# Two layers of a hybrid backbone on one core: the first weight pieces converted earlier, tokens handed on in smaller parts, the last product and the last norm reordered

## The reference

```python
mod = jax.nn.silu(c) @ w_ada[l] + b_ada[l]            # one row of 6 * 1024 numbers per stream
sh1, sc1, g1, sh2, sc2, g2 = jnp.split(mod, 6, axis=-1)
out, k, v, h_fin = token_mixer(x * (1 + sc1) + sh1, ...)   # h @ w_in, then attention, SSD scan, gMLP
x = layer_norm(DEEPNORM_ALPHA * x + g1 * out, ln_g[l, 0], ln_b[l, 0])
ff = hier_moe(x * (1 + sc2) + sh2, ...)               # 32 experts, D_FF 256
x = layer_norm(DEEPNORM_ALPHA * x + g2 * ff, ln_g[l, 1], ln_b[l, 1])

def layer_norm(x, g, b):
    mu = jnp.mean(x, -1, keepdims=True)
    var = jnp.mean(jnp.square(x - mu), -1, keepdims=True)
    return (x - mu) * lax.rsqrt(var + LN_EPS) * g + b
```

## Time and profile before

| | us |
|---|---|
| median of 3 runs | 1404.84 |
| the profiled execution | 1404.46 |
| its span, first to last instruction | 1402.7 |
| PE busy | 1302.7 (93%) |
| DVE busy | 1000.5 (71%) |
| ACT busy | 733.8 (52%) |

### The profile page before, as it was taken

One profiled execution on the slowest core, in us unless ns is written; L12 is line 12 of the kernel. 1 busy time (PEld: TensorE's weight loads), 2 busy tenths in 40 slices (PEclk: granted clock), 3 DMA queues, 4 the chain that ended last, 5 costly groups with the idle time before them and its releaser, 6 DMA issues.

```text
span 1402.7 us, 17438 instructions
## 1 busy us (share of the span) xinstructions
PE 1302.7 (93%) x6480; PEld 1032.3 (74%) x6480; DVE 1000.5 (71%) x1129; ACT 733.8 (52%) x693; POOL 54.5 (4%) x89
## 2 busy tenths in 40 slices
PE   4799999999989999999969999999987999999994
PEld 1668777887677787887757777788776777788873
DVE  0555657667578888888867456666856888888886
ACT  0533543643356666667653444345434666676772
POOL 1301000001000000000020000000000000000000
PEclk8799999989879999999989989899986999999997
DMA  9968653326848989899967667343334898999991
GB/s 358 295 200 304 245 202 128 121 90 230 314 164 303 354 318 333 326 336 342 358 193 238 251 242 258 120 128 100 126 148 143 298 337 320 333 329 330 344 359 49
DMA packets 96275, 349.54 MB, mean 249 GB/s; under 512 B 8580, under 2 KB 12064, under 8 KB 79792
## 3 DMA queue, kind: packets, MB, share of 16 engines
q1 hardware_dynamic: 87216, 295.12, 59.1%
q0 software_dynamic: 8960, 53.16, 10.8%
HBM read 345.58 MB, written 3.70 MB: 249 GB/s over the span
## 4 chain that ended last, share of the span: by engine, by line
PE 70%; DVE 18%; DMA 4%; ACT 3%; issue 2%; DVEq 2%; SPq 1%; ACTq 0%
PE bank L856 66%; DVE wl L1657 9%; PE bank L859 4%; ACT wh L1577 1%; DMA first<-in_w_ada 1%; DMA raw<-in_moe_w 1%; DMA adaw<-in_w_ada 1%; DVE merged L1657 1%; DVE tmp L1657 1%; DVE x L1657 1%; DVE hid L2310 1%; ACT wh L1379 1%; DVE x L1781 0%; DVE gv L1657 0%; DVE xgl L2283 0%
## 5 line engine op out<-in xcount | busy, mean ns | idle before, releaser
L1657 DVE TENSOR_TENSOR wl<-raw,wh 128x2048 fp32r<-128x2048 f32 (+1 forms) x268 | 610.4, 2278 | 129.5 <-ACT wh L1379 66.7
L1577 ACT ACTIVATE wh<-raw 128x2048 fp32r<-128x2048 f32 x192 | 367.3, 1916 | 62.8 <-PE bank L856 47.1
L856 PE MATMUL bank<-wh,xgh 128*128 128x512 f32 x512 | 213.5, 417 | 10.3 <-DVEq L2284 7.0
L856 PE MATMUL bank<-wh,hTh 128*128 128x512 f32 (+1 forms) x480 | 199.2, 415 | 14.3 <-DVE wl L1657 7.6
L856 PE MATMUL bank<-wh,xgl 128*128 128x512 f32 x512 | 205.9, 402 | 0.0
L856 PE MATMUL bank<-wl,xgh 128*128 128x512 f32 x512 | 205.5, 401 | 0.0
L856 PE MATMUL bank<-wl,hTh 128*128 128x512 f32 (+1 forms) x480 | 193.7, 404 | 0.0
L856 PE MATMUL bank<-wh,hTl 128*128 128x512 f32 (+1 forms) x480 | 192.4, 401 | 0.0
L1379 ACT ACTIVATE wh<-raw 128x2048 fp32r<-128x2048 f32 (+1 forms) x76 | 142.2, 1872 | 79.2 <-PE bank L856 72.6
L856 PEld LDWEIGHTS bank<-wh,hTh 128*128 128x128 f32 x480 | 96.5, 201 | 37.3 <-DVE wl L1657 12.6
L856 PEld LDWEIGHTS bank<-wh,xgh 128*128 128x128 f32 x512 | 99.2, 194 | 30.5 <-issue 10.9
(11 more groups left out here) (277 smaller groups left out, 1591.0 us busy)
## 6 DMA issues: line engine op xcount, KB each, us to landing
raw<-in_moe_w SPq DMA_DIRECT2D x256, 512.0 KB, 4.9
raw<-in_moe_w SPq DMA_DIRECT2D x64, 1024.0 KB, 5.6
raw<-in_w_in SPq DMA_DIRECT2D x52, 1024.0 KB, 5.3
adaw<-in_w_ada POOLq DMA_DIRECT2D x32, 1024.0 KB, 7.1
raw<-in_w_branch SPq DMA_DIRECT2D x12, 1024.0 KB, 5.3
raw<-in_w_ada SPq DMA_DIRECT2D x8, 1024.0 KB, 11.1
raw<-in_w_o SPq DMA_DIRECT2D x8, 1024.0 KB, 4.8
first<-in_w_ada SPq DMA_DIRECT2D x4, 1024.0 KB, 16.7
```

The lines of the kernel that those rows point to most:

```text
L856: return behind(nc.tensor.matmul(*args, **kw))
L1577: tally(A_(wh[c][:, :], raw[:, r, :], ACT.Copy), part_high[c])
L1657: return V.tensor_tensor(o, a, b, op)
```

## The change

It has five parts.

1. Layer 0: ACT converts q piece 0 before `take_row` and q piece 1 right behind it, both ahead of the modulation. DVE converts q piece 0 before its modulation and q piece 1 behind the low parts of the first half.
2. The first half of stream 0 is handed on in two parts of two blocks (the diff calls them by first and end): `hT_ready` is raised 5 times a layer, and TensorE waits for the second part only before its third block. In layer 1, DVE puts these two low parts between the statistics of stream 1.
3. The last expert's turned rows have a buffer of their own (`hTTh1`, `hTTl1`), and the columns of `down(30)` are split: the first 512 before `turn_hidden(31)`, the others behind it.
4. Change of layer: ACT converts q piece 0 of layer 1 before it rounds the last expert's rows, not behind it.
5. Last norm: the sum, the mean and the squares of stream 0 are taken by ACT with accumulating activations; DVE works out stream 1's meanwhile, then finishes stream 0 and stream 1. The last operation of each is split in halves of 512 columns, and SP stores the four halves.

One set of statistics is gone from DVE, and both streams are finished in one run at the end. The core of the diff:

```diff
-    sp.wait_ge(out_ready, 1)
-    sp.dma_start(O["y_prompt"][0], x[:, 0, :]).then_inc(out_stored, 16)
-    sp.wait_ge(out_ready, 2)
-    sp.dma_start(O["y_sample"][0], x[:, 1, :]).then_inc(out_stored, 16)
-    sp.wait_ge(out_stored, 32)
+    for s, name in enumerate(("y_prompt", "y_sample")):
+        for h in range(2):
+            hs = slice(h * 512, (h + 1) * 512)
+            sp.wait_ge(out_ready, 2 * s + h + 1)
+            sp.dma_start(O[name][0][:, hs], x[:, s, hs]).then_inc(out_stored, 16)
+    sp.wait_ge(out_stored, 64)
...
     if key[0] == "q":
-        pe.wait_ge(hT_ready, 4 * l + 2 * s + h + 1)
+        pe.wait_ge(hT_ready, 5 * l + (1, 3, 4, 5)[2 * s + h])
     t = bank_free(pe, l, names[s]) if h == 0 else bank[USE[l][names[s]][0]]
     for c in range(4):
+        if key[0] == "q" and s == h == 0 and c == 2:
+            pe.wait_ge(hT_ready, 5 * l + 2)
         ins = mm3(t[:, :], tokens(4 * h + c, s), [i[:, c, :] for i in w], h == 0 and c == 0, h == 1 and c == 3)
...
-    def down(i):
+    def down(i, columns=(0, 1)):
+        last = i == NE - 1
-        for n in range(2):
+        for n in columns:
...
-        ins = mm3(bank[SUM_BANK + n][:, :], [p[:, c, :] for p in (hTTh, hTTl)],
+        ins = mm3(bank[SUM_BANK + n][:, :], [p[last][:, c, :] for p in (hTTh, hTTl)],
...
-    hand_back(("down", i))
+    if 1 in columns:
+        hand_back(("down", i))
...
                 scatter(i // EPG - 1, False)
-            down(i - 1)
+            down(i - 1, (0, 1) if i < NE - 1 else (0,))
         turn_hidden(i)
+    down(NE - 2, (1,))
     down(NE - 1)
...
+            convert_to(0, 0)
+            take_row(0, 0, "ada0")
+            convert_to(0, 1)
+
...
-        frees(ins, f"{which}{s}{h}")
+        if end == 4:
+            frees(ins, f"{which}{s}{h}")
-    def high(s, h):
+    def high(s, first, end):
-            A_(hTh[:, 4 * h:4 * h + 4, s * P:(s + 1) * P],
-               merged[:, s, h * 512:(h + 1) * 512].rearrange("p (c t) -> p c t", c=4), ACT.Copy).then_inc(hT_high, 1)
+            A_(hTh[:, first:end, s * P:(s + 1) * P],
+               merged[:, s, first * P:end * P].rearrange("p (c t) -> p c t", t=P), ACT.Copy).then_inc(hT_high, 1)
-    rows(0, 0)
-    act.drain()
-    high(0, 0)
+    if n == 0:
+        rows(0, 0, 0, 2)
+        act.drain()
+        high(0, 0, 2)
+        rows(0, 0, 2, 4)
+        act.drain()
+        high(0, 2, 4)
+    else:
+        rows(0, 0)
...
     piece(3 * i + 3)
+    if i == NE - 1 and final and l < L - 1:
+        cut[l + 1] = 0
+        convert_to(l + 1, 0)
     act.wait_ge(full[TURN_BANK], loop_uses(TURN_BANK, l, rnd, TURN_USE["hidden", i]))
-    tally(A_(hTTh[:, :, :], bank[TURN_BANK][:, 0:FF].rearrange("p (c t) -> p c t", c=2), ACT.Copy), hidT_high)
+    tally(A_(hTTh[i == NE - 1][:, :, :], bank[TURN_BANK][:, 0:FF].rearrange("p (c t) -> p c t", c=2), ACT.Copy), hidT_high)
     if i and e == 0:
...
-        root_of(1, 1)
+        act.wait_ge(x_last, 1)
+        A_(merged[:, 0, :], x[:, 0, :], ACT.Identity, accum_out=small[:, 0:1])
+        act.drain().then_inc(row_sum, 1)
+        act.wait_ge(row_sum, 1)
+        A_(small[:, 1:2], small[:, 0:1], ACT.Copy, scale=-1.0 / D)
+        act.drain().then_inc(row_mean, 1)
+        act.wait_ge(row_mean, 1)
+        A_(merged[:, 0, :], x[:, 0, :], ACT.Square, bias=small[:, 1:2], accum_out=small[:, 2:3])
+        act.drain().then_inc(squares, 1)
+        square_root(4, l, slice(1, 2))
+        square_root(5, l, slice(0, 1))
...
-                def low(s, h, at=l):
+                LOWS = [(0, 0, 2), (0, 2, 4), (0, 4, 8), (1, 0, 4), (1, 4, 8)]
-                    dve.wait_ge(hT_high, 4 * at + 2 * s + h + 1)
-                    part = (slice(None), slice(4 * h, 4 * h + 4), slice(s * P, (s + 1) * P))
-                    tt(hTl[part], merged[:, s, h * 512:(h + 1) * 512].rearrange("p (c t) -> p c t", c=4), hTh[part].bitcast(F32), ALU.subtract)
+                def low(k, at=l):
+
+                    s, first, end = LOWS[k]
+                    dve.wait_ge(hT_high, len(LOWS) * at + k + 1)
+                    part = (slice(None), slice(first, end), slice(s * P, (s + 1) * P))
+                    tt(hTl[part], merged[:, s, first * P:end * P].rearrange("p (c t) -> p c t", t=P), hTh[part].bitcast(F32), ALU.subtract)
...
-    def finished(s):
-        V.scalar_tensor_tensor(out=x[:, s, :], in0=x[:, s, :], scalar=mean_var[:, s, 0:1], in1=lnrow[:, 0, :],
-                               op0=ALU.subtract, op1=ALU.mult)
+    def finished(s, mean, shifted):
+        V.scalar_tensor_tensor(out=x[:, s, :], in0=x[:, s, :], scalar=mean, in1=lnrow[:, 0, :], op0=shifted, op1=ALU.mult)
+        drain()
+        dve.wait_ge(root_done, 6 * l + 6 - s)
+        V.reciprocal(root[:, s:s + 1], root[:, s:s + 1])
-        V.scalar_tensor_tensor(out=x[:, s, :], in0=x[:, s, :], scalar=root[:, s:s + 1], in1=lnrow[:, 1, :],
-                               op0=ALU.mult, op1=ALU.add)
-        drain().then_inc(out_ready, 1)
+        for h in range(2):
+            hs = slice(h * 512, (h + 1) * 512)
+            V.scalar_tensor_tensor(out=x[:, s, hs], in0=x[:, s, hs], scalar=root[:, s:s + 1], in1=lnrow[:, 1, hs],
+                                   op0=ALU.mult, op1=ALU.add)
+            drain().then_inc(out_ready, 1)
-    spread(0)
-        dve.wait_ge(lnload, 2 * L * 16)
-        invert(0)
-        finished(0)
+        added(0).then_inc(x_last, 1)
+        added(1)
+        sampled(1, 0)
+        sampled(1, 1)
-        invert(1)
-        finished(1)
+        dve.wait_ge(lnload, 2 * L * 16)
+        dve.wait_ge(squares, 1)
+        V.tensor_scalar(root[:, 0:1], small[:, 2:3], 1.0 / D, EPS, ALU.mult, ALU.add)
+        drain().then_inc(var_ready, 1)
+        finished(0, small[:, 1:2], ALU.add)
+        finished(1, mean_var[:, 1, 0:1], ALU.subtract)
+    added(0)
+    sampled(0, 0)
+    sampled(0, 1)
+    spread(0)
...
-    spread(1)
+    added(1)
+    sampled(1, 0)
-        low(0, 0, l + 1)
+        low(0, l + 1)
+    sampled(1, 1)
+    if n:
+        low(1, l + 1)
+    spread(1)
...
-        modulation(l, 0, "adaT0")
-    if l == 0:
-        low(0, 0)
-    else:
-        convert_to(l, 1)
-    low(0, 1)
-    rows("x1T", 0)
-    low(1, 0)
+        modulation(l, 0, "adaT0")
+        low(0)
+        low(1)
-    low(1, 1)
+    low(2)
+    rows("x1T", 0)
+    low(3)
+    low(4)
```

More of the change, by code:

```diff
@@ L489, in hybrid_backbone @@
         out_ready = sem("out_ready")
+        x_last = sem("x_last")
+        row_sum = sem("row_sum")
+        row_mean = sem("row_mean")
+        squares = sem("squares")
         c_exp = sem("c_exp")
@@ L1392, in modulate, with rows @@
                     gain, shift_ = (mod[:, 1], mod[:, 0]) if l == 0 and n == 0 else (affine[n][:, 0], affine[n][:, 1])
-                    def rows(s, h):
+                    def rows(s, h, first=0, end=4):
                         t = bank_full(act, l, f"{which}{s}{h}")
-                        for i in range(4):
+                        for i in range(first, end):
                             c = 4 * h + i
@@ L1412, in modulate @@
                     act.drain().then_inc(s0_act, 1)
-                    high(0, 1)
+                    high(0, 4, 8)
                     rows(1, 1)
```

50 lines of the change are left out of this document (24 added, 26 removed).

## The result

The changed kernel takes 1393.37 us (median of 4 runs, 1391.88 to 1395.73) where the kernel before takes 1404.76 (1403.01 to 1407.28): ratio 0.9926, 95% interval 0.9903 to 0.995. Beside the experiments it was timed again in three more sets: 1393.51, 1393.28 and 1392.14, with ratios 0.9933 [0.9911, 0.9954], 0.9916 [0.9893, 0.9938] and 0.9932 [0.9908, 0.9957]. One of its 22 executions took 1452.26 us at a mean granted clock of 0.814, a slow state of the chip, and is left out of every median. The medians put the change at 11.0 to 11.4 us and the ratios at 9.4 to 11.8; the forecast was 12.3 and 1392.5.

The account below looks back on a forecast made before the run. TensorE bounds the kernel, busy 93% of the span, so only its waits and slow-clock stretches count. Terms 7.9 + 0 + 1.8 + 2.6 = 12.3 us give 1392.5 us; own range 1389.5 to 1395.0, with rivals 1389.0 to 1398.5.

Parts of the forecast that it names:

- Start: Start of layer 0: early q pieces and quarters start TensorE 1.5 us earlier and end q at 53.0; 7.9 us.
- 6 slow matmuls: Start of layer 0: with only 6 matmuls at the slow clock, the term would be 8.3 us.
- Margins of the start: Layer 0: stream 1's first half ready 0.5 us before wanted; q piece 1's conversion ends 0.8 us before ACT is wanted.
- A: Start of layer 0: stream 1's tokens become the wait; term shrinks to about 4 us, time 1396.5; chance 0.20.
- B: After the start: a later load-bound wait takes the gain back, leaving 1 to 2 us of it, 1399; chance 0.12.
- D: Start of layer 0: q piece 1's late load holds ACT and the tokens; slower from a landing at 48; chance 0.03.
- Split: Around the last expert: splitting down(30) only moves TensorE's 1.23 us of idleness ahead of the turn; 0 us per layer.
- Change of layer: Between layers: earlier conversion on ACT gives 0.6 us and quarters start TensorE 1.2 us earlier; together 1.8 us.
- TensorE comes to that half only after 12 slow matmuls (5.1 us) and finds it: Start of layer 1: half 1 is ready when TensorE wants it, although stream 1's later variance delays ACT's root 0.7 us.
- Last norm: End of the program: DVE finishes 2.1 us earlier and the half-size last store gives 0.5; together 2.6 us.
- Rival C: Split of down(30): TensorE's pause before the turn brings back the slow clock, 7 us lost, 1399; chance 0.05.

Follow-up runs that it names:

- first profile: The changed kernel with nothing altered, in its first set against the kernel before; the profiled execution was the slowest of four, 1395.73 us.
- third run: The changed kernel with nothing altered, timed again beside later experiments against the kernel before: 1392.14 us, ratio 0.9932.
- the two kernels with the halves: Changed kernel with hid before the last low part, that part in column halves: 1390.21 us; the same plus stream 1's low part behind its variance: 1388.49 us.

## Why the prediction was right

The forecast was 12.3 us by four terms; the places give 7.5 + 0 + 1.3 + 2.2 = 11.0, and the medians 11.0 to 11.4.

**Start: 7.9 forecast, 6.9 to 7.8 measured.** The mechanism was right and alone gives 6.8 (only the two pieces early). The quarters start TensorE 0.93 us earlier by the clean comparison, 1.2 from before to after, where I had 1.5: two blocks took 0.81 as forecast and `hTh` 0.42 for 0.39, but TensorE came 0.38 us behind the end of the first low part (39.84 to 40.22), more than my 0.1 for semaphores. The step that was missing is a second wait. The first q product goes into the bank in which stream 0's turned rows lie, and ACT gives it back only when it has read all four blocks, with the second pair of `merged` (39.28 + 0.79 = 40.07). In all eleven profiles with quarters TensorE starts 0.14 or 0.15 us behind that and 0.37 to 0.39 behind the end of the low part; with halves it starts 0.13 behind the low part. So the bank and not the low part sets the start, and costs 0.25 us. I let the slow stretch move along with the start and took 5.0 us for it; the eleven profiles have 3.1 to 5.7, in the mean 4.4, the three with halves 4.0 to 4.4, which bears that out, and q taken is 7.2 to 8.3 us earlier in them, 7.7 in the mean. (One number of that part is off: with 6 slow matmuls my rows give 8.5 and not 8.3, held by half 1 at 43.9.)

**Margins of the start.** Stream 1's first half was there in time: ACT waited for DVE's rows as forecast (1.73 us), and TensorE never waited between the first q product and q taken. q piece 1 had landed when ACT came to it (0.17 us of waiting). Rivals A, B and D did not happen in any profile: the 6.8 us of the pieces alone stand in the median as 6.6.

**Split: 0 forecast, 0.00 measured**, by the kernel without it. The reason given was the right one, and it can be turned to use: the pause is DVE's, and the kernel with the last low part in halves takes the sum 1.48 us earlier in layer 1.

**Change of layer: 1.8 forecast.** At the first q product 1.66 us came (turn+16.50 and 16.49 against 18.16), from 0.74 us at the root (turn+11.11 against 11.85; I had 0.6) and 0.93 of quarters (I had 1.2). But the step "TensorE comes to that half only after 12 slow matmuls (5.1 us) and finds it, since DVE's q piece 1 isn't ready before 723.1 anyway" failed: the quarters' low parts between DVE's statistics made DVE's own chain longer (the low part of half 1 starts 11.2 us behind the root, in the kernel before and in the one without quarters 9.9), and TensorE waits up to 1.24 us for half 1. What I had not priced at all is the wait behind that one, for stream 1's first half: it sets TensorE in layer 1 in every profile, 14.87 to 15.27 us behind the root with quarters and 15.29 to 15.94 without, so that 1.3 to 1.5 us are left when q is taken (0.85 to 1.0 against the kernel with only the pieces, which has 35.01 for 35.46). Taking the first wait away gave nothing while the second stood. The late table load took 0.3 to 0.8 us of the gain back in four of the profiles, and the slow clock 1.5 in one.

**Last norm: 2.6 forecast, 2.2 measured.** DVE gives 1.6 where I had 2.1. The term mis-sized is the half operations: 0.75 us each with 0.12 of drain behind, 1.62 for two, not the 0.69 with 0.08 that I took from another kind of operation. That is 0.3 of the 0.5 that is missing; the rest is small: stream 0's variance starts 0.13 later than I had it, and I set DVE's end against SP's issue. The half store gives 0.6 for 0.5 (2.48 us from DVE's end to the span's end, before 3.11). ACT's passes were 1.06 and 1.15, less than the 1.26 that I had bounded them by.

**Rival C**, that the pause brings the slow clock back, was seen in one of the fourteen last turns in the seven profiles of kernels with the pause ahead of the turn: 1.46 us in layer 0 of the first profile (`ygh` at turn+4.85 for +3.39). There the last load was late as well (ACT waited 1.53 us for it, and TensorE 1.96 at the turn, not 1.36), so the pause was longer than the one I had priced. The length alone does not decide it as far as these rows go: a pause of 1.89 us in the last layer of the third run left the sum at turn+3.38.

## What to carry to other kernels

A pause of the matmul engine costs itself and the slow stretch behind it: here 3.5 us of waiting were worth 6.8. Work that takes the wait off one product pays nothing while the same queue's next item is late: compare the second wait (`hTTl`, or stream 1's rows) and not the first (`hid`, or stream 0's second half), and halve the operation that stands in between. When an operand comes earlier, ask also what else the product needs: here the bank. Put a piece of the next stage only where nothing that is wanted sooner stands behind it; ACT's early conversion held `hTTh` by 0.6 and 1.1 us in the two kernels with the halves, where `hTTh` had become the one that counts. And read a gain behind a start at the slow clock from several profiles, since the slow stretch differs by 2.6 us between executions of the same start.
